# Expert loop: u parts one step earlier, v and w parts released tile by tile

## The reference

```python
def peer_ffn(h, peer_wq, peer_keys, peer_u, peer_v):
    x = h.reshape(t, d)
    q = (x @ peer_wq).reshape(t, PEER_HEADS, 2, PEER_DHALF)
    sc = jnp.einsum('thcd,hcnd->thcn', q, peer_keys)
    ...   # top 16 of 16384 experts for each token and head: eidx, gate
    def block(args):
        u = peer_u[eb]
        a = jax.nn.gelu(jnp.einsum('thkd,td->thk', u, xb))
        wgt = a * gb
        return jnp.einsum('thk,thkd->td', wgt, peer_v[eb])
```

## Time and profile before

| what | value |
|---|---|
| time, median of 3 runs (lowest to highest) | 5005.16 us (5004.92 to 5009.96) |
| the profiled execution's own time | 5007.78 us |
| its span | 5006.0 us |
| PE busy | 4198.0 us, 84% of the span |
| DVE busy | 3155.8 us, 63% |
| ACT busy | 1736.2 us, 35% |
| POOL busy | 1391.9 us, 28% |
| mean granted TensorE clock | 0.921 |

### The profile page before, as it was taken

One profiled execution on the slowest core, in us unless ns is written; L12 is line 12 of the kernel. 1 busy time (PEld: TensorE's weight loads), 2 busy tenths in 40 slices (PEclk: granted clock), 3 DMA queues, 4 the chain that ended last, 5 costly groups with the idle time before them and its releaser, 6 DMA issues. The chain is left out here.

```text
span 5006.0 us, 64200 instructions
## 1 busy us (share of the span) xinstructions
PE 4198.0 (84%) x21706; PEld 3734.1 (75%) x21706; DVE 3155.8 (63%) x5125; ACT 1736.2 (35%) x2506; POOL 1391.9 (28%) x992
## 2 busy tenths in 40 slices
PE   8869798646799999999897797886467999999997
PEld 6669677546688888888776796775466888888887
DVE  3464334599677777777735543336896777777776
ACT  2242222109543343333322322221094334334333
POOL 0143101155322322322201531112553232232231
PEclk9989899879899999999998898998798999999999
DMA  3100212105877777777531003120058777777775
GB/s 116 47 9 1 101 59 72 34 1 131 249 261 244 242 251 242 251 246 243 198 104 42 9 1 110 64 67 26 1 140 270 247 245 251 244 247 249 239 249 196
DMA packets 458568, 750.34 MB, mean 150 GB/s; under 512 B 241232, under 2 KB 278864, under 8 KB 458192
## 3 DMA queue, kind: packets, MB, share of 16 engines
q1 hardware_dynamic: 384720, 480.40, 29.5%
q0 software_dynamic: 73728, 268.47, 15.8%
HBM read 696.35 MB, written 52.43 MB: 150 GB/s over the span
## 5 line engine op out<-in xcount | busy, mean ns | idle before, releaser
L123 PE MATMUL banks<-act_hi,exp_uT_hi 128*128 128x384 f32 x2048 | 742.8, 363 | 183.6 <-DVE exp_uT_lo L1994 183.6
L1913 POOL DMA_INDIRECT exp_u_gathered<-in_peer_u,row_experts x256 | 390.3, 1525 | 1601.3 <-DVE exp_row_a L1999 1532.3
L124 PE MATMUL banks<-act_hi,exp_uT_lo 128*128 128x384 f32 x2048 | 732.7, 358 | 0.0
L125 PE MATMUL banks<-act_lo,exp_uT_hi 128*128 128x384 f32 x2048 | 732.4, 358 | 0.0
L124 PE MATMUL banks<-exp_v_hi,exp_w_lo 128*128 128x512 f32 x1536 | 598.4, 390 | 0.0
L123 PE MATMUL banks<-exp_v_hi,exp_w_hi 128*128 128x512 f32 x1536 | 598.1, 389 | 0.0
L125 PE MATMUL banks<-exp_v_lo,exp_w_hi 128*128 128x512 f32 x1536 | 597.7, 389 | 0.0
L123 PEld LDWEIGHTS banks<-act_hi,exp_uT_hi 128*128 128x128 f32 x2048 | 416.2, 203 | 208.1 <-DVE exp_uT_lo L1994 205.6
L124 PEld LDWEIGHTS banks<-act_hi,exp_uT_lo 128*128 128x128 f32 x2048 | 416.4, 203 | 2.4
L125 PEld LDWEIGHTS banks<-act_lo,exp_uT_hi 128*128 128x128 f32 x2048 | 415.2, 203 | 0.0
L1972 ACT CAST exp_v_hi<-exp_v_raw 128x1024 fp32r<-128x1024 f32 x256 | 268.0, 1047 | 355.1 <-PE banks L125 354.7
(11 more groups left out here) (386 smaller groups left out, 8295.8 us busy)
## 6 DMA issues: line engine op xcount, KB each, us to landing
exp_uT_raw<-in_peer_uT SPq DMA_DIRECT2D x260, 512.0 KB, 4.2
exp_v_raw<-in_peer_v SPq DMA_DIRECT2D x256, 512.0 KB, 4.3
exp_gates<-dense_gates SPq DMA_DIRECT2D x256, 192.0 KB, 2.7
win_project_raw<-in_w_in SPq DMA_DIRECT2D x32, 1024.0 KB, 5.5
dense_gates<-gate_block SPq DMA_DIRECT2D x6, 4096.0 KB, 20.7
wkv_project_raw<-in_w_xkv SPq DMA_DIRECT2D x16, 1024.0 KB, 5.0
wpq_project_raw<-in_peer_wq SPq DMA_DIRECT2D x16, 1024.0 KB, 5.1
dense_gates<-last_gates SPq DMA_DIRECT2D x4, 4096.0 KB, 20.7
```

The lines of the kernel that those rows point to most:

```text
L123: pe.matmul(out, lhs[0], rhs[0], start=first, stop=False)
L124: pe.matmul(out, lhs[1], rhs[0], start=False, stop=False)
L125: return pe.matmul(out, lhs[0], rhs[1], start=False, stop=last)
L1913: pool.indirect_dma_start(out, None, table, bass.IndirectOffsetOnAxis(SL.row_idx[:, slot:slot + 1], 0)).then_inc(done, 16)
```

## The change

The semaphore `v_and_w_used` (`vw`) is new. PE raises it behind tiles 0, 1 and 2 of half 1 of the second product, so that ACT may overwrite the parts of these tiles before the whole product is done. ACT and DVE get a new order: the v parts of tiles 0 and 1 stand at the head of a group, those of tiles 2 and 3 inside the steps of tiles 0 and 1; the u parts of tile e+2 stand at the head of the step of tile e, before its gelu; in the last step the u parts stand between gelu and w_hi. The first of the four row products moves into the step of tile 2. PE's own order and SP's and POOL's rows stay.

```diff
         @b.tensor
         def _(pe):
             pe.sem_inc(am, 1)
             pe.sem_inc(om, 1)
+            pe.sem_inc(vw, GROUP - 1)
...
                             if e == GROUP - 1:
                                 i.then_inc(om, 1)
+                            elif half == 1 and t == DENSE - 1:
+                                i.then_inc(vw, 1)
...
+            def gelu(n, e):
+                act.wait_ge(am, n + 2)
+                act.wait_ge(wlo, n + 1)
+                act.activation(w[:, e % 2], PS[:, 2 + e % 2, 0:DTOK], ACT.Gelu_apprx_tanh).then_inc(ge, 1)
...
             with act.Fori(0, NG) as g:
-                for e in range(GROUP):
-                    n = g * GROUP + e
-                    act.wait_ge(v_in[e % 2], g * 32 + (e // 2) * 16 + 16)
+                n = g * GROUP
+                for e in range(2):
+                    act.wait_ge(vw, g * (GROUP - 1) + e + 1)
+                    v_hi(g, e)
+                for e in range(GROUP - 1):
+                    act.wait_ge(am, n + e + 2)
+                    u_hi(n + e + 2, e % 2)
+                    gelu(n + e, e)
                     if e == 0:
-
+                        act.wait_ge(vw, g * (GROUP - 1) + GROUP - 1)
+                        v_hi(g, 2)
+                    if e == 1:
                         act.wait_ge(om, g * NO + 1)
-                    act.copy(vh[:, e], vr[:, e % 2]).then_inc(vho, 1)
-                    if e:
-                        act.wait_ge(am, n + 1)
-                        u_hi(n + 1, (e + 1) % 2)
-                    act.wait_ge(am, n + 2)
-                    act.wait_ge(wlo, n + 1)
-                    act.activation(w[:, e % 2], PS[:, 2 + e % 2, 0:DTOK], ACT.Gelu_apprx_tanh).then_inc(ge, 1)
-                    act.wait_ge(wo, n + 3)
-                    act.copy(wh[:, e], w[:, e % 2]).then_inc(who, 1)
-                act.wait_ge(am, g * GROUP + GROUP + 1)
-                u_hi(g * GROUP + GROUP + 1, 1)
-                act.wait_ge(rd, g * GROUP + GROUP)
+                        v_hi(g, 3)
+                    w_hi(n + e, e)
+                gelu(n + GROUP - 1, GROUP - 1)
+                u_hi(n + GROUP + 1, 1)
+                w_hi(n + GROUP - 1, GROUP - 1)
+                act.wait_ge(rd, n + GROUP)
...
             with dve.Fori(0, NG) as g:
...
+                n = g * GROUP
+                v_lo(n, 0)
+                v_lo(n + 1, 1)
+                for e in range(GROUP - 1):
+                    u_lo(n + e + 2, e % 2)
+                    gated(g, n + e, e)
+                    if e < 2:
+                        v_lo(n + e + 2, e + 2)
+                    else:
+                        row_product(g, 0)
+                    w_lo(n + e, e)
+                gated(g, n + GROUP - 1, GROUP - 1)
+                u_lo(n + GROUP + 1, 1)
+                w_lo(n + GROUP - 1, GROUP - 1)
+                for e in range(1, GROUP):
+                    row_product(g, e)
```

More of the change, by code:

```diff
@@ L1845, in expert_stage @@
         ad = st.sem("output_bank_added")
+        vw = st.sem("v_and_w_used")
         rd = st.sem("row_products_summed")
@@ L1964, in _, with v_hi, w_hi @@
             u_hi(1, 1)
-            with act.Fori(0, NG) as g:
-                for e in range(GROUP):
-                    n = g * GROUP + e
-                    act.wait_ge(v_in[e % 2], g * 32 + (e // 2) * 16 + 16)
+            def v_hi(g, e):
+                act.wait_ge(v_in[e % 2], g * 32 + (e // 2) * 16 + 16)
+                act.copy(vh[:, e], vr[:, e % 2]).then_inc(vho, 1)
+            def gelu(n, e):
+                act.wait_ge(am, n + 2)
+                act.wait_ge(wlo, n + 1)
+                act.activation(w[:, e % 2], PS[:, 2 + e % 2, 0:DTOK], ACT.Gelu_apprx_tanh).then_inc(ge, 1)
+            def w_hi(n, e):
+                act.wait_ge(wo, n + 3)
+                act.copy(wh[:, e], w[:, e % 2]).then_inc(who, 1)
+            with act.Fori(0, NG) as g:
+                n = g * GROUP
[6 more added lines that the diff above has]
+                    gelu(n + e, e)
                     if e == 0:
+                        act.wait_ge(vw, g * (GROUP - 1) + GROUP - 1)
+                        v_hi(g, 2)
+                    if e == 1:
                         act.wait_ge(om, g * NO + 1)
-                    act.copy(vh[:, e], vr[:, e % 2]).then_inc(vho, 1)
-                    if e:
-                        act.wait_ge(am, n + 1)
-                        u_hi(n + 1, (e + 1) % 2)
-                    act.wait_ge(am, n + 2)
-                    act.wait_ge(wlo, n + 1)
-                    act.activation(w[:, e % 2], PS[:, 2 + e % 2, 0:DTOK], ACT.Gelu_apprx_tanh).then_inc(ge, 1)
-                    act.wait_ge(wo, n + 3)
-                    act.copy(wh[:, e], w[:, e % 2]).then_inc(who, 1)
-                act.wait_ge(am, g * GROUP + GROUP + 1)
-                u_hi(g * GROUP + GROUP + 1, 1)
-                act.wait_ge(rd, g * GROUP + GROUP)
+                        v_hi(g, 3)
[4 more added lines that the diff above has]
+                act.wait_ge(rd, n + GROUP)
                 act.activation(rg[:], ra[:], ACT.Gelu_apprx_tanh).then_inc(rge, 1)
@@ L2017, in _, with v_lo, gated, w_lo @@
             u_lo(1, 1)
-            with dve.Fori(0, NG) as g:
[L2019 to L2034, removed]
+            def v_lo(n, e):
+                dve.wait_ge(vho, n + 1)
+                dve.tensor_tensor(vl[:, e], vr[:, e % 2], vh[:, e].bitcast(F32), ALU.subtract).then_inc(vlo, 1)
+            def gated(g, n, e):
+                dve.wait_ge(ge, n + 3)
+                dve.wait_ge(g_in[e % 2], g * 32 + (e // 2) * 16 + 16)
+                dve.tensor_tensor(w[:, e % 2], w[:, e % 2], gt[:, e % 2], ALU.mult).then_inc(wo, 1)
+            def w_lo(n, e):
+                dve.wait_ge(who, n + 1)
+                dve.tensor_tensor(wl[:, e], w[:, e % 2], wh[:, e].bitcast(F32), ALU.subtract).then_inc(wlo, 1)
+            with dve.Fori(0, NG) as g:
+                n = g * GROUP
[14 more added lines that the diff above has]
+                    row_product(g, e)
                 dve.wait_ge(rge, g + 1)
```

## The result

The changed kernel takes 5321.88 us in the median of 4 runs (5319.71 to 5333.45), the kernel before 5005.52 us beside it: slower by a ratio of 1.0635 (95% interval 1.0616 to 1.0653). Forecast were 5317 us.

The account below looks back on a forecast made before the run. PE, waiting 2.3 us a group for u_lo, bounds the kernel. 60 later groups at 4.2 us more (252 us) plus 60 us for first groups on 5007.8 give 5320, less 2.6: 5317 us; range 5195 to 5430.

Parts of the forecast that it names:

- The wait at tile 2 goes: PE's first products: u_lo of tile 2 written at T + 6.8, before PE comes at T + 8.5; the 2.28 us stall goes.
- Gated 1.04 us later, T + 8.0: DVE's gated of tile 0: moved back by u_hi of tile 2, from T + 6.97 to T + 8.0.
- The ring of load, u_hi, u_lo, gated, SP, 7.3 us a step: Each step: gated issues the following u load, a closed chain costing landing + 3.6 us, 7.3 us with 3.7 us landing.
- The last u_hi ahead of w_hi: Last step: third load delays w_lo of tile 3 to T + 29.9; PE waits 3.4 us at tile 3 of half 0.
- The early v parts, 0 to 0.1 us: v parts of tiles 0 and 1 beside the second product, where ACT was idle: 0 to 0.1 us a group.
- The row product ahead of w_lo of tile 2, 0: DVE's 1.2 us before w_lo of tile 2: ready T + 24.4, PE comes T + 24.5; covered, cost 0.
- The clock, 1.4 us for a fall: PE behind a wait: part of the work runs at 1.2 GHz instead of 2.4, costing 1.4 us a fall.
- The first two groups: Each layer's start, where SP also stores gates: steps of 10.4 us, 16.7 and 13.4 us more, 60 us over two layers.
- The mean of later groups: Groups after each layer's first two: 41.5 against 37.36 us, 0.1 off both for the clock, 4.2 us more, 60 such groups.
- The page's transfer time: DMA of 512 KB: about 2.0 us plus bytes over 436 GB/s gives 3.2 us; by it, a group takes 40.0 us.
- The load of the earlier trace that I called isolated: A u load landing in 3.3 us, taken as having no other traffic behind or ahead of it but its gates.
- The rival with no wait at all, 4781 us: Expert loop: PE never waits, 33.7 us a group, 224 us less, 4781 us; chance 0.05.

Follow-up runs that it names:

- cutting it on SP: Changed kernel with SP loading the gates of tile n+1, not n+2, after the v load of tile n+2: 4773.25 us, ratio 0.9534 to the kernel before.
- cutting it between u_hi and gelu on ACT and DVE: Changed kernel with gelu ahead of u_hi and gated ahead of u_lo in the first three steps, SP unchanged: 4853.79 us, ratio 0.9690 to the kernel before.
- the halved load: Changed kernel with each u load in the loop bringing 256 KB instead of 512, the rest stale: 5112.9 us, ratio 1.0211 to the kernel before.
- Putting the last u parts back: Changed kernel with a group's last u_hi and u_lo behind the last w_hi and w_lo, SP unchanged: 5157.84 us, ratio 1.0295 to the kernel before.
- the v half: Kernel before with only the early v_hi and v_lo and the new PE counter; u parts, row product and SP as before: 5147.54 us, ratio 1.0272.
- the u half alone: Kernel before with only the u parts moved as in the change; v parts, first row product and SP as before: 5275.32 us, ratio 1.0538.
- the u half with v loads and gates one tile later: Kernel before with only the u parts moved, and SP loading v and gates of tile n+1 behind u of n+2: 4764.29 us, ratio 0.9513.
- an edit that removed the v wait: Changed kernel with last u parts behind w_hi and w_lo, v parts of tiles 2 and 3 one step later, row products at the end: 5261.11 us.

## Why the prediction was right

- *The wait at tile 2 goes*: right. Three first products run on, and the first wait is at tile 3.
- *Gated 1.04 us later, T + 8.0*: measured T + 8.07; the load's issue, T + 8.8, at T + 8.83.
- *The ring of load, u_hi, u_lo, gated, SP, 7.3 us a step*: steps of 7.4 and 7.3 us in the mean of 29 groups, with 3.8 us from a load's issue to u_hi (I had taken 3.7). That it is this ring is shown from three sides: cutting it on SP (4773 us), cutting it between u_hi and gelu on ACT and DVE (4854 us), and the halved load, whose landing counts threefold.
- *The last u_hi ahead of w_hi*: the last w_lo started at 2143.75, so it was written at T + 29.7 (forecast 29.9); PE's wait there was 2.72 us (3.4). PE came later than I had reckoned: tile 3's first product took 5.87 us (2129.46 to 2135.33) instead of 5.6. The second product's tiles 0 to 2 then ran at the 0.681 us of my sum. Putting the last u parts back gave about half of the loss, so the term is real. But the sum that I made for that kernel, 5010 us, missed by 148: the chain through v_lo of tile 0 and the v load comes up at once when this one goes.
- *The early v parts, 0 to 0.1 us*: too low, and the price was made for tiles 0 and 1 only; tiles 2 and 3 had none. In the changed kernel the v half and the moved row product together cost 0.5 us a group and 47 us in all (against the u half alone); by themselves, with SP unchanged, the v half cost 136 us. Which part of it costs the 0.5 us is not shown.
- *The row product ahead of w_lo of tile 2, 0*: covered in 23 of the 29 later groups; in the other 6 PE waited at tile 2 of half 0, for 0.2 to 1.5 us.
- *The clock, 1.4 us for a fall*: after the second wait the 45 matmuls took 11.7 to 12.0 us in 16 of the 29 later groups, 10.3 to 10.4 in 9 and 12.7 to 13.2 in 4. So a fall mostly cost 1.4 to 1.7 us, but in 4 groups more (in the group of 1445.99 PE stayed at 1.2 GHz for over 5 us), and in 9 groups waits of 1.1 to 3.6 us brought none. The mean was 11.6 us, as in my sum, because these balanced; that is luck.
- *The first two groups*: the first took 1352.92 - 1285.81 = 67.1 us against 51.0, 16.1 more (forecast 16.7); the second 51.3 (forecast 50.8). This came out partly by luck. The steps were 9.4 and 9.6 us instead of 10.4 and the last w_lo came 0.7 us early in the second group (1.7 in the first), while the 45 matmuls behind it took 12.8 us instead of 11.6.
- *The mean of later groups*: from 1404.18 to 2610.06 us 29 periods, 41.6 us (forecast 41.4).
- *The page's transfer time* of the Trainium skill (DMA: Bandwidth & Descriptors, Anatomy of one DMA), an estimate of 3.2 us by its fit, is near the fastest landing here (3.2 us in the changed kernel, 3.1 before); the median was 3.8 us and the slowest 7.1. That page of the Trainium skill makes the fit for transfers issued by GpSimd, and these were issued by SP. The load of the earlier trace rows that I called isolated wasn't: a v load was issued 2.24 us behind it, before it had landed. The same page of the Trainium skill says under Rules for kernel authors to issue a DMA early and wait for it late. The runs bear that out: at 4.9 us a landing, loads issued early enough cost nothing.

The rival with no wait at all, 4781 us, was the time that the change could have had: 4773 us were measured once SP's gates stood one tile later, and 4764 us for the u half with v loads and gates one tile later.

## What to carry to other kernels

Work that is moved earlier on a compute engine moves its demand for data earlier too; before moving it, find the issue of that load in its queue's row and what that queue waits for ahead of it. If the issue stands behind a result of the very step that now starts with the load's data, the two form a ring, and every landing is paid in full. Order a load queue by when its buffers come free and are wanted, and put the loads with the latest release last.

## What the runs showed that I had not expected

A wait for one part is often a cover for another. With the u ring weakened but not cut, waits for v loads and for DVE's end of group took its place (39.0 and 40.9 us a group), and an edit that removed the v wait made the kernel 103 us slower. Only orders in which both kinds of load were there in time for PE reached 33.3 us. And the landing of the same 512 KB of u went from 3.4 us to 6.4 us within the group of the changed kernel shown above; the slow one was issued at 2140.14, 2.0 us behind a v load. That the load ahead slows it is likely and not shown, as no run changed only that.
